# A ten-sublayer transformer on one core: the last two output slots of each sublayer in four quarters, and the next input prepared by token halves

## The chip, the cores and the metric

One core of one Trainium2 chip runs the whole program. The metric is the device time in microseconds (us) of one execution. The core has TensorE (PE, with its weight loads PEld), VectorE (DVE), ScalarE (ACT), GpSimd (POOL) and SyncE (SP, which here only issues DMAs).

## The reference

256 tokens of width 1024 pass through ten sublayers. Each ends in the same way: a product with an output weight matrix, a residual and a layer norm.

```python
for i in range(DEPTH):                       # sublayers 0 to 3
    h = x * (1.0 + scale) + shift            # modulation from c
    y = windowed_gqa(...) if i == 0 else recurrent_block(...)
    x = layer_norm(DN_ALPHA * x + (1.0 + gate) * y, ln_g[i, 0], ln_b[i, 0])
    y = sq_relu_mlp(x * (1.0 + scale) + shift, mlp_w1[i], mlp_w2[i])
    x = layer_norm(DN_ALPHA * x + (1.0 + gate) * y, ln_g[i, 1], ln_b[i, 1])
for i in range(DEPTH):                       # sublayers 4 to 9
    x = layernorm(DN_ALPHA_2 * x + 0.5 * swiglu(x, ...), ...)
    x = layernorm(DN_ALPHA_2 * x + hybrid_mixer(x, ...), ...)
    x = layernorm(DN_ALPHA_2 * x + 0.5 * swiglu(x, ...), ...)
```

So sublayer 0 is attention, 2 a recurrence, 1 and 3 are MLPs, 5 and 8 mixers, and 4, 6, 7 and 9 gated MLPs. "Boundary s" is the place between sublayer s and s + 1.

## The kernel before

**Precision by parts.** Every large product is made of three: each operand is split into a high part (rounded) and a low part (what is left), and `mm3` (L490 to L492) multiplies high by high, low by high and high by low. ScalarE makes the high part of the weights (`weights_hi`, L948) and VectorE the low part (`weights_lo`, L1289), one slot of up to 128 x 2048 at a time.

**Slots.** All weights come in numbered slots. SyncE loads them into three raw buffers; three high and three low buffers follow. A slot is 48 matmuls over 256 columns (`cols_slot`, which needs the transposed input) or 24 over 512 (`rows_slot`, which adds into `y_rows`, 256 tokens as two halves t of 128). High parts are made two slots ahead, but at the end of a sublayer only the next sublayer's first slot is made before the norm; its second and third come after the input's preparation, since ScalarE and VectorE work in the order in which the program is written.

**The end of a sublayer.** `rows_slot` of the last slot runs half 0 (twelve matmuls) and then half 1, and signals `y_half` between them. `norm` on VectorE takes each half: in sublayers 0 to 3 a product with the gate (L1455) and a sum with the scaled residual `x_scaled` (L1457), otherwise one operation (L1459); then statistics (L1463, L1465), a sum with the epsilon and a reciprocal (L1466, L1467). ScalarE takes the root and scales half 0 (L1083 to L1089); VectorE scales half 1 (L1470).

**The preparation of the next input** (`prep`). TensorE transposes the rows (L581), eight blocks of 128 x 128 for each half, into four banks that hold both halves. Banks 0 and 2 are modulated by VectorE (L1390, 256 columns each time), 1 and 3 by ScalarE (L990). ScalarE makes the high part in four pieces (L996), VectorE the low part in four (L1382, `xl_ready` 0 to 3). The first slot goes through its products by input block and waits for each `xl_ready`.

**GpSimd** makes `x_scaled` for the next residual, three operations over 128 x 1024 for each half (L1787, L1789, L1791), as soon as that half's rows are ready (`xn_ready0`, `xn_ready1`). At boundary 0 these lie between loads of the modulation's weights.

**The modulation.** In sublayers 0 and 1 VectorE also accumulates the product of c with the weights `ada_w` (L1339), and TensorE sums it over partitions (`ada_reduce`, L556). In `mlp(1)` the last of these stands at i = 16. Sublayer 2 begins on VectorE with 20 small operations on `rnn_decay_cols` (96 x 32) that wait for each other, with one exponential on ScalarE among them; the low weights of its second slot stand behind them.

Of the kernel before, what the change touches and what calls it, by code (L numbers as in the profile page):

```python
# [27 lines left out]
P = 128  # L28
S = 256
# [67 lines left out]
def build(nc, I, C, out, counts, n_sub):  # L97
# [5 lines left out]
    with ctx:  # L103
# [68 lines left out]
        pos["at"] += 64  # L172
        hid_at = pos["at"]
# [23 lines left out]
        XTF = put("xt", [P, KC, S], at=hid_at)  # L197
# [271 lines left out]
        def _(pe):  # L469
# [51 lines left out]
            def rows_slot(label, lh, ll, k0, first, last, s):  # L521

                n, wh, wl = open_slot(label)
                for t in range(NT):
                    for kk in range(2):
                        xa, xb = lh(k0 + kk)[:, t * P:(t + 1) * P], ll(k0 + kk)[:, t * P:(t + 1) * P]
                        for h in range(2):
                            ins = mm3(Y[:, t, h * 512:(h + 1) * 512], xa, xb, wh[:, kk, h * 512:(h + 1) * 512],
                                      wl[:, kk, h * 512:(h + 1) * 512], first and kk == 0, last and kk == 1)
                    if last and t == 0:  # L530
                        ins.then_inc(*inc("y_half", s))
                ins.then_inc(*inc("rows_done", label))

# [6 lines left out]
            def xready(s):  # L540
                seen = set()

                def f(k):
                    if k // 2 not in seen:
                        seen.add(k // 2)
                        pe.wait_ge(*past("xl_ready", (s, k // 2)))
                return f
# [22 lines left out]
            def prep(s):  # L570

                banks = [topen(("xt", s, e), "AD"[e % 2 == 0]) for e in range(4)]
                for t in range(NT):
                    if s > 0:
                        pe.wait_ge(*past(f"xn_ready{t}", (s - 1, t)))
                    elif t == 0:
                        pe.wait_ge(*past("x_in"))
                    for e in range(4):
                        for kk in range(2):
                            k = 2 * e + kk  # L580
                            ins = pe.transpose(banks[e][:, kk * S + t * P:kk * S + (t + 1) * P], XN[:, t, k * P:(k + 1) * P],  # L581
                                               IDN[:, :])
                        if t == 1:
                            ins.then_inc(*inc("tile_done", ("xt", s, e)))
# [12 lines left out]
            prep(0)  # L597
# [65 lines left out]
            for i in range(4):  # L663
                if i == 1:
                    ada_reduce(5)
                rows_slot((0, "out", i), lambda k: OH[:, k, :], lambda k: OL[:, k, :], 2 * i, i == 0, i == 3, 0)
# [19 lines left out]

            def hidden_rows(s, i, n):
# [3 lines left out]
                hh, hl = HH[:, i % 2, :], HL[:, i % 2, :]  # L691
                rows_slot((s, "w2", i), lambda k: hh.rearrange("p (a b) -> p a b", a=2)[:, k],
                          lambda k: hl.rearrange("p (a b) -> p a b", a=2)[:, k], 0, i == 0, i == n - 1, s)
# [10 lines left out]

            def between(s):

                if s + 1 < n_sub:
                    prep(s + 1)

            def recurrence(s):  # L710
# [4 lines left out]
                for i in range(12):  # L715
# [14 lines left out]
                    if g >= 0:  # L730
                        pe.wait_ge(*past("yl", g))
                        if g == 0:
                            y_wait(s)
                        rows_slot((s, "out", g), lambda k: YH[:, g % 4, k, :], lambda k: YL[:, g % 4, k, :], 0, g == 0, g == 7, s)

            def mixer(s):
# [180 lines left out]
                for i in range(4):  # L917
# [3 lines left out]
                    rows_slot((s, "out", i), lambda k: XH[:, k, :], lambda k: XL[:, k, :], 2 * i, i == 0, i == 3, s)  # L921

            between(0)
            for s in range(1, n_sub):
# [8 lines left out]
                between(s)  # L933
# [3 lines left out]
        def _(act):  # L937
# [42 lines left out]
            def prep(s):  # L980
# [4 lines left out]
                def modulate(e):  # L985

                    bank = tile(("xt", s, e))
                    for kk in range(2):
# [967 lines left out]
```

## Time and profile before

| | |
|---|---|
| median of 3 runs | 2641.73 us (2641.48 to 2643.64) |
| span of the profiled execution | 2640.4 us |
| TensorE busy | 2375.5 us, 90% |
| TensorE weight loads | 2143.8 us, 81% |
| VectorE busy | 1675.4 us, 63% |
| ScalarE busy | 1117.3 us, 42% |
| GpSimd busy | 498.6 us, 19% |
| mean granted clock of TensorE | 0.935 |

The profiled execution's own time is its span and what lies around it. The chain of work that ended last is TensorE for 73% and VectorE for 21% of the span. In the tables below a time is the start from the beginning of the span, and the second number is how long the instruction or the group (xN) took; in brackets stands how long the engine was idle before it, and what ended that.

### The profile page before, as it was taken

The numbers are of one execution on the slowest core, as the hardware profiler recorded it, in microseconds if no ns is written. First come the engines' busy times: TensorE is split into PE (matmuls) and PEld (weight loads), VectorE is DVE, ScalarE is ACT, GpSimd is POOL, SyncE is SP. The second block draws the span as 40 slices with busy tenths as digits, with TensorE's granted clock in tenths as the row PEclk, the third lists the DMA queues.
The fourth block names the chain that finished last, engine by engine and source line by source line (L and its number), as shares of the span: only waits on it lengthen the run. The fifth ranks groups of instructions, "written<-read, shape, count | busy, mean of one in ns | idle before, by whom it ended". The sixth has DMA issues, their size and how long they took to land.

```text
span 2640.4 us, 37438 instructions
## 1 busy us (share of the span) xinstructions
PE 2375.5 (90%) x15755; PEld 2143.8 (81%) x15755; DVE 1675.4 (63%) x1946; ACT 1117.3 (42%) x1452; POOL 498.6 (19%) x379
## 2 busy tenths in 40 slices
PE   4879997886999899899899889999989899889998
PEld 4668887764898899888698789989988778788997
DVE  6977765798655644599544564464467964447544
ACT  2334433665444444455333344343445553234343
POOL 2112113332200200345022020020032522112000
PEclk9889998888899899999898999999999998898999
DMA  9768873223455456545221155555564442013652
GB/s 321 250 210 275 291 244 93 84 76 103 163 188 176 161 187 180 163 129 138 67 65 49 66 174 190 178 172 179 191 142 152 127 115 64 23 59 128 209 186 101
DMA packets 304282, 400.47 MB, mean 152 GB/s; under 512 B 43215, under 2 KB 262969, under 8 KB 304116
## 3 DMA queue, kind: packets, MB, share of 16 engines
q1 hardware_dynamic: 283360, 336.75, 40.2%
q0 software_dynamic: 17504, 57.89, 6.9%
q10 hardware_dynamic: 3252, 3.45, 0.4%
q8 instruction: 125, 2.05, 0.3%
q14 instruction: 41, 0.34, 0.0%
HBM read 393.86 MB, written 4.19 MB: 151 GB/s over the span
## 4 chain that ended last, share of the span: by engine, by line
PE 73%; DVE 21%; ACT 3%; issue 2%; DMA 1%; POOL 0%; SPq 0%; ACTq 0%; DVEq 0%; POOLq 0%
PE tiles L490 14%; PE tiles L491 14%; PE tiles L492 14%; PE y_rows L490 6%; PE y_rows L491 6%; PE y_rows L492 6%; DVE conv_qkv_t L1609 3%; DVE weights_lo L1289 3%; PE tiles L845 2%; PE tiles L859 2%; PE tiles L855 1%; PE tiles L829 1%; DVE xt_lo L1382 1%; DVE ada_acc L1339 1%; DVE rnn_conv_out L1548 1%
## 5 line engine op out<-in xcount | busy, mean ns | idle before, releaser
L1289 DVE TENSOR_TENSOR weights_lo<-weights_raw,weights_hi 128x2048 fp32r<-128x2048 f32 (+2 forms) x316 | 740.2, 2347 | 530.3 <-ACT weights_hi L948 529.9
L490 PE MATMUL tiles<-xt_hi,weights_hi 128*128 128x256 f32 (+1 forms) x3216 | 930.4, 289 | 33.0 <-DVE xt_lo L1382 24.5
L491 PE MATMUL tiles<-xt_lo,weights_hi 128*128 128x256 f32 (+1 forms) x3216 | 921.2, 286 | 0.0
L492 PE MATMUL tiles<-xt_hi,weights_lo 128*128 128x256 f32 (+1 forms) x3216 | 920.3, 286 | 0.0
L948 ACT ACTIVATE weights_hi<-weights_raw 128x2048 fp32r<-128x2048 f32 (+2 forms) x316 | 593.0, 1880 | 218.6 <-PE y_rows L492 191.2
L490 PEld LDWEIGHTS tiles<-xt_hi,weights_hi 128*128 128x128 f32 (+1 forms) x3216 | 621.7, 193 | 52.0 <-issue 38.2
L491 PEld LDWEIGHTS tiles<-xt_lo,weights_hi 128*128 128x128 f32 (+1 forms) x3216 | 622.0, 193 | 3.3
L492 PEld LDWEIGHTS tiles<-xt_hi,weights_lo 128*128 128x128 f32 (+1 forms) x3216 | 621.1, 193 | 0.0
L490 PE MATMUL y_rows<-weights_hi,hid_hi 128*128 128x512 f32 x608 | 244.0, 401 | 0.0
L491 PE MATMUL y_rows<-weights_lo,hid_hi 128*128 128x512 f32 x608 | 242.7, 399 | 0.0
L492 PE MATMUL y_rows<-weights_hi,hid_lo 128*128 128x512 f32 x608 | 242.5, 399 | 0.0
L1787 POOL TENSOR_TENSOR x_scaled<-x_rows,ln_gb_rows 128x1024 f32<-128x1024 f32 x18 | 44.5, 2474 | 873.9 <-ACT x_rows L1089 873.1
L952 ACT ACTIVATE hid_act<-tiles 128x512 f32<-128x512 f32 x76 | 45.5, 598 | 277.6 <-PE tiles L492 277.6
L490 PEld LDWEIGHTS y_rows<-weights_hi,hid_hi 128*128 128x128 f32 x608 | 115.8, 191 | 33.6 <-issue 6.0
L1914 POOL TENSOR_TENSOR l_level_t<-l_t,levels_t 128x512 f32<-128x512 f32 x56 | 76.1, 1359 | 344.2 <-DVE a_t L1682 200.3
L492 PEld LDWEIGHTS y_rows<-weights_hi,hid_lo 128*128 128x128 f32 x608 | 115.5, 190 | 28.3
L491 PEld LDWEIGHTS y_rows<-weights_lo,hid_hi 128*128 128x128 f32 x608 | 115.3, 190 | 25.0
L1339 DVE SCALAR_TENSOR_TENSOR ada_acc<-ada_ring,c_cols,ada_acc 128x1024 f32<-128x1024 f32 x84 | 108.5, 1292 | 17.3 <-DMA ada_ring<-in_ada_w_dram 12.5
L1609 DVE SCALAR_TENSOR_TENSOR conv_qkv_t<-conv_in,conv_cols,conv_qkv_t 128x256 f32<-128x256 f32 x144 | 104.5, 766 | 7.7 <-ACT conv_qkv_t L1169 5.8
L1038 ACT ACTIVATE hid_hi<-hid_val 128x512 fp32r<-128x512 f32 x44 | 27.8, 632 | 181.1 <-DVE hid_val L1508 181.1
L1825 POOL DMA_DIRECT2D ada_ring<-in_ada_w_dram x76 | 40.7, 535 | 267.6 <-DVE ada_acc L1339 221.3
L581 PE MATMUL tiles<-ident,x_rows 128*128 128x128 f32 x160 | 34.8, 391 | 49.7 <-ACT x_rows L1089 27.8
(334 smaller groups left out, 3320.5 us busy)
## 6 DMA issues: line engine op xcount, KB each, us to landing
weights_raw<-in_ffn_w_dram SPq DMA_DIRECT2D x132, 1024.0 KB, 5.1
weights_raw<-in_mlp_w_dram SPq DMA_DIRECT2D x64, 1024.0 KB, 5.8
weights_raw<-in_w_in_dram SPq DMA_DIRECT2D x52, 1024.0 KB, 5.4
ada_ring<-in_ada_w_dram POOLq DMA_DIRECT2D x76, 512.0 KB, 4.9
weights_raw<-in_rnn_w_in_dram SPq DMA_DIRECT2D x16, 768.0 KB, 4.8
ada_ring<-in_ada_w_dram SPq DMA_DIRECT2D x20, 512.0 KB, 7.7
weights_raw<-in_w_in_dram SPq DMA_DIRECT2D x32, 256.0 KB, 4.4
weights_raw<-in_w_branch_a_dram SPq DMA_DIRECT2D x32, 256.0 KB, 4.6
```

What stands on the lines that cost most here:

```text
L490: pe.matmul(o, a, c, start=first, stop=False)
L491: pe.matmul(o, a, d, start=False, stop=False)
L492: return pe.matmul(o, b, c, start=False, stop=last)
L845: ins = pe.matmul(bank[:, j * P:(j + 1) * P], MM[:, c, j, :], TT[:, c, j, :], start=True, stop=True)
L859: ins = pe.matmul(bank[:, j * P:(j + 1) * P], XX[:, c, j, :], UU[:, c, j, :], start=True, stop=True)
L948: act.activation(slot_view(WHI, m, NSPL), slot_view(RAW, m, NRAW), ACT.Copy).then_inc(*inc("hi_ready", m))
L952: act.activation(dst, src, func, **kw).then_inc(*inc("free_A", label))
L1289: dve.tensor_tensor(slot_view(WLO, m, NSPL), slot_view(RAW, m, NRAW), slot_view(WHI, m, NSPL).bitcast(F32), ALU.subtract).then_inc(*inc("l ...
L1339: ins = dve.scalar_tensor_tensor(ACC[:, t % 3, :], ADR[:, m % NADR, :], CC[:, kc:kc + 1], ACC[:, t % 3, :], ALU.mult, ALU.add)
L1609: ins = dve.scalar_tensor_tensor(CB[:, ct, :], CIN[:, j % 2, jj, tap:tap + S], w, CB[:, ct, :], ALU.mult, ALU.add)
L1787: chain(pool.tensor_tensor(XS[:, t, :], XN[:, t, :], GB[:, 0, :], ALU.mult))
L1914: pool.tensor_tensor(MM[:, c, :, :], LT[:, c, :, :], lev, ALU.mult).then_inc(*inc("m_ready", (k_, i, c)))
```

## The change

1. `rows_slot` is used for all output slots but the last two of a sublayer, a and b. These go through `rows_tail`: a and b of half 0 (then `y_half`), a and b of half 1's first 512 columns (`y_third`), a of its other 512 columns, the transposes of half 0, b of those columns, the transposes of half 1. The last two slots' inputs are therefore waited for at other places: in `mlp` and `ffn` nothing of the slot before the last is run until the loop's last turn, and in `mlp(1)` the last `ada_reduce` stands ahead of both.
2. `prep` works by halves: each half has one bank of four blocks for ScalarE and one for VectorE, modulated in pieces of 128 columns; high and low parts are made in four pieces by half and by four blocks. `xl_ready` has two steps, each after the piece of half 1.
3. `norm`: ScalarE takes the root of variance plus epsilon (a new constant), VectorE the reciprocal, and VectorE scales both halves. Half 1's residual and statistics are made in two pieces of 512 columns. VectorE's preparation stands behind half 1's norm; ScalarE's part for half 0 stands ahead of half 1's root. In the last sublayer scaling, gain and shift are two operations for each half.
4. GpSimd's copies wait for the last `xl_ready` of the next sublayer.
5. `xt` lies 8 KB further on, clear of the hidden layer's parts.

```diff
             def rows_slot(label, lh, ll, k0, first):
...
+            def rows_tail(s, a, b, b_ready):
+
+                la, lb = a[0], b[0]
+                for h in range(2):
+                    rows_part(*a, False, False, 0, h)
+                b_ready()
+                for h in range(2):
+                    ins = rows_part(*b, False, True, 0, h)
+                ins.then_inc(*inc("y_half", s))
+                rows_part(*a, False, False, 1, 0)
+                rows_part(*b, False, True, 1, 0).then_inc(*inc("y_third", s))
+                rows_part(*a, False, False, 1, 1).then_inc(*inc("rows_done", la))
+                if s + 1 < n_sub:
+                    prep(s + 1, 0)
+                rows_part(*b, False, True, 1, 1).then_inc(*inc("rows_done", lb))
+                if s + 1 < n_sub:
+                    prep(s + 1, 1)
...
             def hidden_rows(s, i, n):
-                pe.wait_ge(*past("hid_ready", (s, i)))
+
+                if i < n - 1:
+                    pe.wait_ge(*past("hid_ready", (s, i)))
                 if i == 0:
                     y_wait(s)
...
+                if i < n - 2:
+                    rows_slot(*hidden(s, i), i == 0)
+                elif i == n - 1:
+                    rows_tail(s, hidden(s, i - 1), hidden(s, i), lambda: pe.wait_ge(*past("hid_ready", (s, i))))
...
             def prep(s):
...
+                modulate(s, 0)
+                x_lo(s, 0, 0)
+                modulate(s, 1)
+                x_lo(s, 1, 0)
+                x_lo(s, 0, 1)
+                x_lo(s, 1, 1)
...
             def norm(s):
...
+                residual(s, 0, 0, D)
+                for h in range(2):
+                    ins = dve.bn_stats(ST[:, 0, h, :], XN[:, 0, h * 512:(h + 1) * 512])
+                chain(ins)
+                variance(s, 0)
+                scale_rows(s, 0)
+                dve.wait_ge(*past("y_third", s))
+                residual(s, 1, 0, 512)
+                dve.bn_stats(ST[:, 1, 0, :], XN[:, 1, 0:512]).then_inc(*inc("ln_part", s))
+                dve.wait_ge(*past(*y_end[s]))
+                residual(s, 1, 512, D)
+                dve.wait_ge(*past("ln_part", s))
+                chain(dve.bn_stats(ST[:, 1, 1, :], XN[:, 1, 512:D]))
+                variance(s, 1)
+                scale_rows(s, 1)
                 if s + 1 < n_sub:
                     prep(s + 1)
...
             def scaled(s):
 
                 pool.wait_ge(*past("gb_in", s))
+                pool.wait_ge(*past("xl_ready", (s + 1, 1)))
```

**On TensorE at the end of sublayer 1.** The hidden layer's last block, the position of the modulation's reduction (`ones,ada_acc`) and the two output slots. Before:

```order
L683 MATMUL tiles<-bucket_hot,rel_bias 128x384
L490 MATMUL y_rows<-weights_hi,hid_hi 128x512
L491 MATMUL y_rows<-weights_lo,hid_hi 128x512
L492 MATMUL y_rows<-weights_hi,hid_lo 128x512
...
L556 MATMUL tiles<-ones,ada_acc 128x1 x8
L490 MATMUL y_rows<-weights_hi,hid_hi 128x512
...
L581 MATMUL tiles<-ident,x_rows 128x128 x16
L490 MATMUL tiles<-xt_hi,weights_hi 96x256
```

After:

```order
L708 MATMUL tiles<-bucket_hot,rel_bias 128x384
L582 MATMUL tiles<-ones,ada_acc 128x1 x8
L491 MATMUL y_rows<-weights_hi,hid_hi 128x512
L492 MATMUL y_rows<-weights_lo,hid_hi 128x512
...
L606 MATMUL tiles<-ident,x_rows 128x128 x8
L491 MATMUL y_rows<-weights_hi,hid_hi 128x512
...
L606 MATMUL tiles<-ident,x_rows 128x128 x8
L491 MATMUL tiles<-xt_hi,weights_hi 96x256
```

The reduction moved from between the two output slots to ahead of both, and six output matmuls now stand between the two groups of transposes.

**On VectorE at boundary 1,** from half 1's statistics to the start of sublayer 2's decay columns. Before:

```order
L1463 BN_STATS ln_stats<-x_rows 128x6
L1465 BN_AGGR ln_mean_var<-ln_stats 128x2 [waits dve_chain]
L1466 TENSOR_SCALAR ln_rstd<-ln_mean_var 128x1 [waits dve_chain]
L1467 RECIPROCAL ln_rstd<-ln_rstd 128x1 [waits dve_chain]
L1470 TENSOR_SCALAR x_rows<-x_rows,ln_mean_var,ln_rstd 128x1024 [waits ln_rstd]
L1390 TENSOR_SCALAR xt<-tiles,prep_scale,prep_shift 128x256 [waits tile_done]
L1390 TENSOR_SCALAR xt<-tiles,prep_scale,prep_shift 128x256
L1390 TENSOR_SCALAR xt<-tiles,prep_scale,prep_shift 128x256 [waits tile_done]
L1390 TENSOR_SCALAR xt<-tiles,prep_scale,prep_shift 128x256
L1382 TENSOR_TENSOR xt_lo<-xt,xt_hi 128x512 [waits xh_ready] x4
L1531 TENSOR_SCALAR rnn_decay_cols<-rnn_gate_cols 96x32
```

After:

```order
L1538 BN_STATS ln_stats<-x_rows 128x6 [waits ln_part,dve_chain]
L1505 BN_AGGR ln_mean_var<-ln_stats 128x2 [waits dve_chain]
L1510 RECIPROCAL ln_rstd<-ln_rstd 128x1 [waits ln_std]
L1513 TENSOR_SCALAR x_rows<-x_rows,ln_mean_var,ln_rstd 128x1024 [waits dve_chain]
L1418 TENSOR_SCALAR xt<-tiles,prep_scale,prep_shift 128x128 [waits tile_done]
L1418 TENSOR_SCALAR xt<-tiles,prep_scale,prep_shift 128x128 x3
L1426 TENSOR_TENSOR xt_lo<-xt,xt_hi 128x4x128 [waits xh_ready]
L1418 TENSOR_SCALAR xt<-tiles,prep_scale,prep_shift 128x128 [waits tile_done]
L1418 TENSOR_SCALAR xt<-tiles,prep_scale,prep_shift 128x128 x3
L1426 TENSOR_TENSOR xt_lo<-xt,xt_hi 128x4x128 [waits xh_ready] x3
L1595 TENSOR_SCALAR rnn_decay_cols<-rnn_gate_cols 96x32
```

The modulations became eight of half the width, and one low piece stands among them; the decay columns follow directly on the last low piece, as before.

## Rows read from the trace of the kernel before

**Rows 1.** waits of TensorE: engine, tile, line <- released by: us in all, times, longest

```profile
PE tiles L581 <- ACT x_rows L1089: 27.8, 9, 3.8
PE tiles L490 <- DVE xt_lo L1382: 24.5, 10, 3.7
PE tiles L490 <- DVE weights_lo L1289: 7.4, 5, 4.2
```

**Rows 2.** timeline at boundary 4: start us, us, engine, line, operation

```profile
1057.65 1.23 DVE L1459 SCALAR_TENSOR_TENSOR x_rows<-y_rows,x_scaled 128x1024 f32<-128x1024 f32 x1 [2.92 <-PE y_rows L492]
...
1060.01 0.40 PE L492 MATMUL y_rows<-weights_hi,hid_lo 128*128 128x512 f32 x1
1060.23 0.21 DVE L1465 BATCH_NORM_AGGREGATE ln_mean_var<-ln_stats 128x2 f32<-128x12 f32 x1
...
1064.19 1.62 DVE L1470 TENSOR_SCALAR x_rows<-x_rows,ln_mean_var,ln_rstd 128x1024 f32<-128x1024 f32 x1 [0.27 <-ACT ln_rstd L1083]
1065.86 1.97 PE L581 MATMUL tiles<-ident,x_rows 128*128 128x128 f32 x8 [1.03 <-DVE x_rows L1470]
...
1069.83 0.55 PE L490 MATMUL tiles<-xt_hi,weights_hi 128*128 128x256 f32 x1 [2.00 <-DVE xt_lo L1382]
...
1078.49 0.39 PE L490 MATMUL tiles<-xt_hi,weights_hi 128*128 128x256 f32 x1 [1.26 <-DVE weights_lo L1289]
```

**Rows 3.** stretch 1069 to 1073: us; busy (instructions) of each engine; clock; DMA; GB/s

```profile
1069.00:1073.00 4.00, 3.17 (x15) 3.20 (x16) 3.75 (x4) 4.00 (x7) 3.92 (x2) 0.50 0.02 4
```

**Rows 4.** timeline of GpSimd and VectorE at boundary 5

```profile
1550.75 2.77 POOL L1791 TENSOR_SCALAR x_scaled<-x_scaled 128x1024 f32<-128x1024 f32 x1
1551.23 1.10 DVE L1382 TENSOR_TENSOR xt_lo<-xt,xt_hi 128x512 fp32r<-128x512 f32 x1
1553.60 2.52 POOL L1787 TENSOR_TENSOR x_scaled<-x_rows,ln_gb_rows 128x1024 f32<-128x1024 f32 x1
1553.79 2.88 DVE L1382 TENSOR_TENSOR xt_lo<-xt,xt_hi 128x512 fp32r<-128x512 f32 x1
```

**Rows 5.** groups by line and shape: busy us, mean ns of one | idle before

```profile
L1707 DVE TENSOR_SCALAR x_level<-tiles,g_cols 128x128 f32<-128x128 f32 x32 | 8.6, 341 | 0.0
L1390 DVE TENSOR_SCALAR xt<-tiles,ln_cols 128x256 f32<-128x256 f32 x24 | 11.4, 536 | 4.7 <-PE tiles L581 4.7
L990 ACT ACTIVATE xt<-tiles,ln_cols 128x256 f32<-128x256 f32 x24 | 12.2, 562 | 18.5 <-PE tiles L581 18.5
```

**Rows 6.** timeline at boundary 1

```profile
387.60 2.67 DVE L1339 SCALAR_TENSOR_TENSOR ada_acc<-ada_ring,c_cols,ada_acc 128x1024 f32<-128x1024 f32 x2
392.06 1.17 PE L556 MATMUL tiles<-ones,ada_acc 128*128 128x1 f32 x10
...
419.25 0.70 DVE L1531 TENSOR_SCALAR rnn_decay_cols<-rnn_gate_cols 96x32 f32<-96x32 f32 x1
...
427.96 0.53 PE L490 MATMUL tiles<-xt_hi,weights_hi 128*96 128x256 f32 x1 [4.21 <-DVE weights_lo L1289]
```

**Rows 7.** timeline at boundary 0

```profile
163.75 2.67 DVE L1339 SCALAR_TENSOR_TENSOR ada_acc<-ada_ring,c_cols,ada_acc 128x1024 f32<-128x1024 f32 x2
...
177.62 1.97 PE L581 MATMUL tiles<-ident,x_rows 128*128 128x128 f32 x8 [2.35 <-DVE x_rows L1470]
```

**Rows 8.** timeline at boundaries 2 and 3

```profile
650.65 1.23 DVE L1455 TENSOR_TENSOR x_rows<-y_rows,gate_rows 128x1024 f32<-128x1024 f32 x1 [2.78 <-PE y_rows L492]
662.72 1.97 PE L581 MATMUL tiles<-ident,x_rows 128*128 128x128 f32 x8 [3.62 <-DVE x_rows L1470]
...
851.63 1.23 DVE L1455 TENSOR_TENSOR x_rows<-y_rows,gate_rows 128x1024 f32<-128x1024 f32 x1 [3.01 <-PE y_rows L492]
863.70 1.97 PE L581 MATMUL tiles<-ident,x_rows 128*128 128x128 f32 x8 [3.62 <-DVE x_rows L1470]
```

**Rows 9.** timeline at the start and at the end

```profile
49.49 0.55 PE L490 MATMUL tiles<-xt_hi,weights_hi 128*128 128x256 f32 x1 [1.66 <-DVE xt_lo L1382]
...
2636.01 1.22 DVE L1478 TENSOR_TENSOR x_rows<-x_rows,ln_gb_rows 128x1024 f32<-128x1024 f32 x1
```

More of the change, by code:

```diff
@@ L172, in build @@
         pos["at"] += 64
+        EPS = put("ln_eps", [P, 1])
         hid_at = pos["at"]
@@ L519, in v_slot, with rows_slot @@
                 ins.then_inc(*inc("tile_done", label))
-            def rows_slot(label, lh, ll, k0, first, last, s):
+            def rows_slot(label, lh, ll, k0, first):
                 n, wh, wl = open_slot(label)
@@ L596, in _ @@
                 ada_reduce(t)
-            prep(0)
+            for t in range(NT):
+                prep(0, t)
             for i in range(6):
@@ L916, in mixer @@
                     cols_slot((s, "bb", i), OH, OL, "D", ready=(lambda k: pe.wait_ge(*past("olb_ready", (s, k // 2)))) if i == 0 else None)
-                for i in range(4):
+                for i in range(3):
                     pe.wait_ge(*past("ml_ready", (s, i)))
@@ L932, in _ @@
                     ffn(s)
-                between(s)
         @block.scalar
@@ new lines, in residual @@
+            def residual(s, t, c0, c1):
+                x, y = XN[:, t, c0:c1], Y[:, t, c0:c1]
+                last = c1 == D
+                if s < 4:
+                    dve.tensor_tensor(x, y, GATE[:, c0:c1], ALU.mult).then_inc(*(inc("y_free", (s, t)) if last else inc("y_gated", (s, t))))
+                    dve.wait_ge(*past(*(("y_free", (s, t)) if last else ("y_gated", (s, t)))))
+                    chain(dve.tensor_tensor(x, x, XS[:, t, c0:c1], ALU.add))
+                else:
+                    ins = dve.scalar_tensor_tensor(x, y, 1.0 if is_mix(s) else 0.5, XS[:, t, c0:c1], ALU.mult, ALU.add)
+                    if last:
+                        ins.then_inc(*inc("y_free", (s, t)))
+                        dve.wait_ge(*past("y_free", (s, t)))
+                    else:
+                        chain(ins)
@@ new lines, in variance, with scale_rows @@
+            def variance(s, t):
+                dve.bn_aggr(MV[:, t, :], ST[:, t, :, :].rearrange("p a b -> p (a b)")).then_inc(*inc("ln_var", (s, t)))
+            def scale_rows(s, t):
+                dve.wait_ge(*past("ln_std", (s, t)))
+                chain(dve.reciprocal(RV[:, t, 0:1], RV[:, t, 1:2]))
+                x = XN[:, t, :]
+                if s + 1 < n_sub:
+                    dve.tensor_scalar(x, x, MV[:, t, 0:1], RV[:, t, 0:1], ALU.subtract, ALU.mult).then_inc(*inc(f"xn_ready{t}", (s, t)))
+                else:
+                    chain(dve.scalar_tensor_tensor(x, x, MV[:, t, 0:1], GB[:, 0, :], ALU.subtract, ALU.mult))
+                    dve.scalar_tensor_tensor(x, x, RV[:, t, 0:1], GB[:, 1, :], ALU.mult, ALU.add).then_inc(*inc("out_rows", t))
@@ L1471, in norm @@
                 if s + 1 < n_sub:
                     prep(s + 1)
-                else:
-                    dve.wait_ge(*past("gb_in", s))
-                    for t in range(NT):
-                        dve.wait_ge(*past(f"xn_ready{t}", (s, t)))
-                        chain(dve.tensor_tensor(XN[:, t, :], XN[:, t, :], GB[:, 0, :], ALU.mult))
-                        dve.tensor_tensor(XN[:, t, :], XN[:, t, :], GB[:, 1, :], ALU.add).then_inc(*inc("out_rows", t))
             def lo_hidden(s, i):
@@ L1776, in _ @@
             chain(pool.memset(ESEL[:, :], 0.0))
+            chain(pool.memset(EPS[:, :], LN_EPS))
             pool.memset(ESEL[:, 15:16], 1.0).then_inc(*inc("ones_ready"))
```

187 lines of the change are left out of this document (88 added, 99 removed).

## The prediction

> **What bounds the kernel now.** TensorE is busy for 90% of the span, so a change off its path is worth nothing, and one on it is worth what TensorE waited. I read the views in this order. First the waits of TensorE [rows 1]: of its idle time 27.8 us stand in front of the transposes of the normalised rows and 24.5 us in front of a sublayer's first matmul, both at the nine places where one sublayer ends and the next begins; 7.4 us stand in front of a second slot whose low weights are late. Then one such place in order of time, 4 to 5 [rows 2]: from the last output matmul (1060.01) to the first matmul of the next sublayer (1069.83) lie 9.8 us, a chain of small steps on VectorE and ScalarE, and then the second slot waits until 1078.49. Then the clock there [rows 3]: the first slot after the pause runs at 0.50 of full speed, the 1.2 GHz level, after an engine that had mostly waited since 1060.4.
>
> **The lock.** GpSimd's copies (six of about 2.5 us at each boundary) and VectorE's reads exclude each other [rows 4]: the low part of the input started at 1553.79 while a GpSimd tensor_tensor ran from 1553.60 to 1556.12, and ended at 1556.67, though it takes 0.65 alone. Under GpSimd's tensor_scalar (from 1550.75) the same operation took 1.10: this form blocks only in pieces. The Trainium skill (SBUF — State Buffer, "Who interferes with whom") says that the loser of this port fully blocks for the whole instruction; by that rule, the trace agrees for tensor_tensor and not for tensor_scalar.
>
> **Boundaries 4 to 8 (no gate).** Count from the start S of the last two slots: 48 matmuls at 0.233 us, so S = 1060.01 - 47 x 0.233 = 1049.05. Before, the chain of half 0 starts at 8.6 [rows 2], after 36 matmuls; now after 24, at 5.8. VectorE has its last weights work done 2.9 before 1057.65, at 5.7: just free. The chain takes 2.58 to the variance [rows 2], then 0.21, root 0.24, reciprocal 0.21, scaling 0.85 (the row's 1.62 has a wait for GpSimd in it, which is now silent): 4.1, so 9.9. TensorE has run 42 matmuls by then (9.8): no wait. Eight transposes 1.0, the last six matmuls 1.4: the last starts at 12.1, not 11.0. Half 1's first columns are done meanwhile; its second columns start 0.45 later and take 0.7 residual, 0.7 statistics, 0.24, 0.24, 0.21, 0.85: rows ready at 15.5, where before they were at 16.8 (1065.86).
> Then the preparation. It now has 4 + 4 modulations of 128 columns for each half. VectorE's 256-column form takes 536 ns and a 128-column one 341 [rows 5]; back to back I take 1.2 for four. ScalarE's 562 ns has no 128-column row: between half of it and all of it; I take 0.39 each back to back, 1.56 for four, since its fixed part stays. The chain is VectorE modulation of half 0 (1.2), ScalarE high part (0.65), ScalarE modulation of half 1 (1.5), high part (0.65), VectorE low part (0.7), TensorE (0.15): 4.85, against 3.97 before. First matmul at 20.35 against 20.8: **0.4 less**, five times, 2.2. The second slot's wait for low weights, 7.4 in all less 4.2 at boundary 1 [rows 1, 6], goes: 3.2 more. It should go because the high part is ready 6.5 after the transposes start and a copy holds VectorE until 8.6, so low weights are there at 10.8, and TensorE needs them at 12 to 13.4 (its first slot takes 7.1 to 8.6 at these clocks). Sum **-5.4**.
>
> **Boundary 3 (gate, free GpSimd contention before).** The gate adds 1.26 to the chain of half 0 (5.4) and makes half 1's tail 4.15. S = 851.63 - 8.6 = 843.03 [rows 8]. Rows 0 at 11.2, so TensorE waits 1.4; last matmul 13.35; rows 1 at 17.5 = 860.5, against 863.70. The preparation took 5.7 before, with copies running through it; now 4.85. **-4.0.**
> **Boundary 2** is held by the recurrence's last step: the chain of half 0 starts at 650.65 in both. Then 656.05, 658.2, 662.35 against 662.72 [rows 8]; with the preparation's 0.8, **-1.2**. Three quarters of the two slots' work now stand behind that step, which eats the rest.
> **Boundary 0.** The chain can't start 2.8 earlier, since VectorE has two accumulations of the modulation until 166.42 [rows 7]: 166.45 + 5.4 + 2.2 + 4.15 = 178.15 against 177.62, and no copies disturbed it before, so its preparation took 3.6: 4.85 now. **+1.8.** At the **start** both halves are turned at once (from 44.2), and the narrower steps put the first matmul at 51.1 instead of 49.49 [rows 9]: **+1.6**.
> **The end.** Scaling and the last weights and biases become two operations for each half instead of three, the first half's done while the second runs: 2622.3 + 3.3 + 2.6 = 2628.2, then 2 x 1.4, 0.7 and 2.6 = 2634.3, against 2637.2 [rows 9]: **-2.9**.
>
> **Boundary 1** is where the change costs. Two things move. (a) TensorE's reduction of the modulation stands ahead of both slots, not between them; it needs the accumulation that ends at 390.27 and ran at 392.06, hidden [rows 6]. Now TensorE waits for it, and S is 390.3 + 1.75 = 392.05; rows 1 at 409.55, the input complete at +6.15 = 415.7. (b) Behind the input VectorE has 20 small dependent operations for the decay columns, then the low weights; from 419.25 to TensorE's restart at 427.96 they took 8.7 [rows 6], with the copies over. Now the copies start at the same moment, and 18 of the 20 read two operands or go in the form that the lock stops. Between two copies passes one of them (0.2), since GpSimd takes the port while the next waits for its predecessor. Step by step from 0: copy to 2.55, one operation, ScalarE's table and exponential to 4.45, copy to 5.4, one; tensor_scalar 5.5 to 8.3, of whose middle 1.2 us are free: six; copy to 10.85, one; copy to 13.65, one; tensor_scalar to 16.5: six; the rest and the low weights (1.76): 18.8. TensorE at 434.5 instead of 427.96: **+6.6**. Bounds: no blocking at all, 423.9, a gain of 4.0; both tensor_scalars blocking throughout, 436.5, +8.6.
>
> **Sum:** 1.6 + 1.8 + 6.6 - 1.2 - 4.0 - 5.4 - 2.9 = -3.5. The profiled execution has a span of 2640.4, and the median of the runs is 2641.7, so 1.3 lie around the span and move with nothing here: **2638.2 us**. GpSimd's own later work (clearing the convolution's input, bias rows) starts some 7 us later at each boundary, several slots before its first reader: I take nothing. Later slots: I followed the lock through four slots and found low weights 1 to 5 us ahead.
>
> **Rivals.**
> *The small operations slip through* (B): if GpSimd lets VectorE go on between copies, boundary 1 gains 4 and the time is 2638.2 - 10.6 = 2627.6. For it: 128x1 operations pass in any case. Against: the row at 1553.79. Chance 0.14.
> *The lock takes the second slot* (C, slower): low weights at each of boundaries 2 to 8 are caught by two copies instead of one, because the port is given to GpSimd again. They then come 2.65 later, at 13.4, or 0.6 after the mean need of 12.8, and each later slot's low weights are as late; with the 3.2 us not gained and one further copy (0.6 x 7 = 4.2, up to 2.6 lost for the ones behind) the time is 2638.2 + 3.2 + 4.2 + 2 = 2647.6. It decides when the low weights are more than 12.8 behind the transposes. Chance 0.15.
> *Narrow is not cheaper* (D): if 128 columns cost as 256 do, 0.7 on VectorE and 0.3 on ScalarE are added at nine preparations: 2647. Against: 341 against 536 ns. Chance 0.06.
> *The page's lock* (E): tensor_scalar blocks throughout and boundary 1 costs 8.6: 2640.2. The sentence of the Trainium skill above states it. Against: the 1.10 us row. Chance 0.10.
> *The clock rises sooner* (F): the transposes and matmuls between the pauses keep the 2.4 GHz level; a first slot lost about 2 us to the lower level, so half of that at eight boundaries gives 2630. For it: TensorE's pauses are now two of 3 us. Against: pauses of 2.5, 1 and 2 us already brought the lower level. Chance 0.10.
> My forecast (A) holds the other 0.45, of which 0.12 lie more than 5.3 us below the median.
>
> **How the numbers follow.** 0.2% (5.3 us) is about what a measurement can tell from no change. Faster: B, F and 0.12 of A, 0.36. Slower: C, D, 0.21, less what of them stays inside, 0.20. Same: 0.44. The range leaves out B's end and C's tail: 2629 to 2647.
>
> **What would show it.** Two transposes of eight with six output matmuls between them, without a wait at 4 to 8 and with 1.4 us at 3. Scaling at 0.81 throughout. At boundary 1 the reduction waiting about 4 us, decay operations strung between copies, and a wait of some 12 us for low weights. No other wait for low weights at a second slot. Wrong would be: first matmuls less than 0 or more than 1.5 us earlier at 4 to 8, or a boundary 1 that is no later.

## The result and the profile after

The changed kernel takes 2647.0 us (median of 20 runs, 2645.5 to 2650.8), the kernel before 2642.6 (20 runs, 2640.6 to 2647.7): ratio 1.0016, 95% interval 1.0009 to 1.0022. That is inside the 0.2% called no change, but slower, where 3.5 us less was forecast, and 0.01 us outside the range. The profiled execution's span is 2645.3, 4.9 longer than before.

The waits of TensorE after (engine, tile, line, releaser: us in all, times, longest) answer to [rows 1]:

```profile
PE tiles L606 <- DVE x_rows L1513: 39.1, 18, 3.9
PE tiles L491 <- DVE xt_lo L1426: 35.1, 10, 3.7
...
PE tiles L491 <- DVE weights_lo L1323: 7.8, 1, 7.8
```

The waits at the boundaries grew (39.1 for 27.8, 35.1 for 24.5), but work stands between them now; the low weights keep TensorE waiting at one place instead of five. Boundary 4 in order of time, the timeline of TensorE, VectorE and GpSimd together (start, us, engine, line, operation), answers to [rows 2]:

```profile
1047.62 0.40 PE L491 MATMUL y_rows<-weights_hi,hid_hi 128*128 128x512 f32 x1
...
1053.29 1.23 DVE L1496 SCALAR_TENSOR_TENSOR x_rows<-y_rows,x_scaled 128x1024 f32<-128x1024 f32 x1
...
1057.51 1.10 PE L606 MATMUL tiles<-ident,x_rows 128*128 128x128 f32 x8 [0.18 <-DVE x_rows L1513]
...
1059.61 0.40 PE L493 MATMUL y_rows<-weights_hi,hid_lo 128*128 128x512 f32 x1
...
1062.27 0.81 DVE L1513 TENSOR_SCALAR x_rows<-x_rows,ln_mean_var,ln_rstd 128x1024 f32<-128x1024 f32 x1
...
1063.14 1.09 PE L606 MATMUL tiles<-ident,x_rows 128*128 128x128 f32 x8 [3.13 <-DVE x_rows L1513]
...
1067.95 0.55 PE L491 MATMUL tiles<-xt_hi,weights_hi 128*128 128x256 f32 x1 [3.72 <-DVE xt_lo L1426]
...
1069.15 2.38 POOL L1852 TENSOR_TENSOR x_scaled<-x_rows,ln_gb_rows 128x1024 f32<-128x1024 f32 x1 [174.26 <-DVE xt_lo L1426]
```

This is the picture that was forecast: eight transposes and six matmuls without a wait worth the name, scaling at 0.81, 4.81 from the transposes to the first matmul (4.85 forecast), copies behind it, no wait in the second slot. And yet two numbers don't fit. Eight transposes were put ahead of the last matmul, but it comes at 1059.61, not later than 1060.01. And what boundaries 2 to 8 gained is gone by the end.

I followed the shift against before from boundary to boundary, at the 240th matmul behind the last transpose of the rows. The last column is a later experiment (the hidden tiles put where they were against 64 bytes).

| part | forecast | after | after_unaligned |
|---|---|---|---|
| start and boundary 0 | +3.4 | +5.2 | +5.0 |
| boundary 1 | +6.6 | +3.7 | +6.8 |
| boundary 2 | -1.2 | -2.5 | -2.0 |
| boundary 3 | -4.0 | -6.8 | -4.4 |
| boundaries 4 to 8 | -5.4 | -14.2 | -9.8 |
| the two mixers (sublayers 5, 8) | 0 | +23.6 | +23.6 |
| end | -2.9 | -4.1 | -3.0 |
| sum | -3.5 | +4.9 | +16.1 |

So the size of the miss isn't 8 us. Two unforeseen terms, -10 and +21, stand against each other. (The mixers' row holds 2 x 1.1 for the later last matmul, which the forecast has at the boundaries. Two expectations below have 3.8 up to sublayer 1 and 5.0 for boundary 1; on the same matmul in both kernels it is 5.2 and 3.7.)

**The mixers.** The stretch from the long wait in front of the attention rows to the last output matmul of sublayer 8, in both kernels (us, busy of PE, PEld, DVE, ACT and POOL with their instructions, granted clock, DMA share, GB/s). Before:

```profile
2028.00:2427.00 399.00, 364.03 (x2521) 324.28 (x2521) 251.83 (x427) 159.62 (x276) 96.16 (x68) 0.92 0.30 91
```

After:

```profile
2029.00:2439.00 410.00, 375.57 (x2529) 334.07 (x2528) 253.38 (x429) 161.68 (x281) 95.12 (x67) 0.90 0.30 89
```

The same work (eight transposes more, about 1 us) keeps TensorE busy 11.5 us longer, at a mean granted clock of 0.90 for 0.92. It doesn't wait longer: the waits for attention rows have the same lengths (the two longest 3.05 and 2.15 us before, 3.06 and 2.15 after) and add up to 26.5 both times. Summed over the clock records, a whole mixer sublayer, the 5th or the 8th, spends 71.7 us at the 1.2 GHz level before and 92.2 after; the 20.5 us between them cost half, 10.3, of the 11.8 that it takes longer from its 240th matmul on. The changed code comes behind all of this: only the tail and GpSimd's times differ ahead of it.

Where the level falls differs, even at the same place of the program and of the span. Before, the first attention matmul behind the long wait, and the stretch at the lower level next to it:

```profile
2028.79 0.90 PE L759 MATMUL y_rows<-ident,probs_a 128*128 128x128 f32 x3 [3.05 <-DVE probs_a L1599]
2028.80:2032.20 3.40, 3.40 (x14) 2.74 (x15) 3.40 (x2) 2.29 (x2) 1.06 (x1) 0.50 0.02 5
```

After:

```profile
2028.80 0.90 PE L794 MATMUL y_rows<-ident,probs_a 128*128 128x128 f32 x3 [3.06 <-DVE probs_a L1663]
2027.30:2034.20 6.90, 5.40 (x23) 4.74 (x24) 6.83 (x9) 3.09 (x7) 2.49 (x2) 0.51 0.20 46
```

Both waits end 2028.8 us into the span. Before, the lower level starts with the first matmul behind the wait (the 6.8 us ahead of it are at 1.00); after, 1.4 us ahead of it, and it stays twice as long.

### The profile page after: what moved, and what is told of

Same layout as the page of the kernel before. It is cut to its first block, busy times and chain, and to the rows that moved or that the text cites. A ratio compares the mean times of both kernels' runs of the same rounds, so it can differ in the third digit from the quotient of the medians.

```text
span 2645.3 us, 37493 instructions
## 1 busy us (share of the span) xinstructions
PE 2375.2 (90%) x15755; PEld 2153.1 (81%) x15755; DVE 1693.3 (64%) x1988; ACT 1116.3 (42%) x1462; POOL 525.3 (20%) x380
## 4 chain that ended last, share of the span: by engine, by line
PE 74%; DVE 19%; ACT 3%; issue 2%; DMA 1%; POOL 0%; SPq 0%; ACTq 0%; DVEq 0%; POOLq 0%
PE tiles L491 15%; PE tiles L492 14%; PE tiles L493 14%; PE y_rows L491 6%; PE y_rows L492 6%; PE y_rows L493 6%; DVE conv_qkv_t L1673 3%; DVE weights_lo L1323 2%; PE tiles L880 2%; PE tiles L894 2%; PE tiles L890 1%; PE tiles L864 1%; DVE ada_acc L1373 1%; DVE rnn_conv_out L1612 1%; DMA ada_ring<-in_ada_w_dram 1%
## 5 line engine op out<-in xcount | busy, mean ns | idle before, releaser
L1323 DVE TENSOR_TENSOR weights_lo<-weights_raw,weights_hi 128x2048 fp32r<-128x2048 f32 (+2 forms) x316 | 767.7, 2434 | 508.5 <-ACT weights_hi L984 508.2
L491 PE MATMUL tiles<-xt_hi,weights_hi 128*128 128x256 f32 (+1 forms) x3216 | 929.0, 289 | 43.9 <-DVE xt_lo L1426 35.1
L1075 ACT ACTIVATE hid_hi<-hid_val 128x512 fp32r<-128x512 f32 x44 | 27.8, 632 | 179.7 <-DVE hid_val L1572 179.7
L1546 DVE TENSOR_TENSOR hid_lo<-hid_val,hid_hi 128x512 fp32r<-128x512 f32 x76 | 57.5, 757 | 32.1 <-ACT hid_hi L1075 30.8
```

The costliest lines, as they stand in the source:

```text
L491: pe.matmul(o, a, c, start=first, stop=False)
L1323: dve.tensor_tensor(slot_view(WLO, m, NSPL), slot_view(RAW, m, NRAW), slot_view(WHI, m, NSPL).bitcast(F32), ALU.subtract).then_inc(*inc("l ...
L1546: dve.tensor_tensor(HL[:, i % 2, :], VB[:, i % 2, :], HH[:, i % 2, :].bitcast(F32), ALU.subtract).then_inc(*inc("hid_ready", (s, i)))
```

## The experiments

Theory A is the forecast's: the order and the lock. G: the late copies put GpSimd's later work in the mixer's way. P: where a mixer's pauses fall against the changes of the granted clock decides its time, not its code. H, formed later: the place of a tile. Each ratio is against the kernel before on the same chip.

**1. The two parts apart.** In the changed kernel the copies are set free again:

```
-                pool.wait_ge(*past("xl_ready", (s + 1, 1)))
...
-                pool.wait_ge(*past("xl_ready", (1, 1)))
```

> The changed kernel without the two waits that keep GpSimd's copies behind the next input: the copies start when the normalised rows are there, as in the kernel before. Theory A (the copies' lock is what boundary 1 pays for, and what the later boundaries gained): boundary 1 loses its 5.0 us again, and boundaries 2 to 8 give back about 1.6 us each (scaling at 1.6 instead of 0.85, low weights late at the second slot), 11 in all; start and end as in the changed kernel. If the mixers keep their longer time (11.8 us each), that gives 2647 + 6 = 2653. Rival G (the mixers are longer because the copies and what follows them on GpSimd run 7 us later in them): the mixers lose 23 us and the time is near 2630. The mixers' time between the boundaries tells them apart: 11.8 longer than before each, or as before.

2660.6 us, 1.0062 (1.0049 to 1.0075), 7.6 more than theory A's 2653: boundary 1 lost its 4.0 us, but boundaries 2 to 8 gave back 15, not 11. And the kernel before with only the copies late (the same two waits, on `xl_ready` 3):

> The kernel before with only the copies moved behind the next input's low part. Theory A: boundary 1 loses about 6 us (decay operations between copies), and boundaries 2 to 8 gain: scaling of half 1 without the lock (0.8), the preparation of boundary 3 without copies (1.5), no late weights at second slots (3.2 in all): about 9 less, so 2642.6 + 6 - 9 = 2640. Rival G: each mixer takes some 12 us longer than before, 2664. Rival P (the mixers' time hangs on where their pauses fall against the changes of the clock, not on the code): mixers anywhere from 0 to 12 us longer, with the same waits.

2640.1 us, 0.9995 (0.9983 to 1.0006). Theory A gave the time, for a wrong reason: without the mixers (+8.3 and +11.9 at the same places) this kernel is 23 us faster, and boundary 1, where 6 was charged, costs 0.4, since its input is ready 4.1 earlier. G falls: the mixers are 11.7 and 12.0 longer with early copies, too. What the copies do when they are early, in the timeline of copies_early at boundary 4:

```profile
1071.92 2.35 POOL L1852 TENSOR_TENSOR x_scaled<-x_rows,ln_gb_rows 128x1024 f32<-128x1024 f32 x1
1074.35 2.71 POOL L1854 TENSOR_TENSOR x_scaled<-x_scaled,ln_gb_rows 128x1024 f32<-128x1024 f32 x1
1077.14 3.10 POOL L1856 TENSOR_SCALAR x_scaled<-x_scaled 128x1024 f32<-128x1024 f32 x1
...
1073.24 5.81 DVE L1426 TENSOR_TENSOR xt_lo<-xt,xt_hi 128x512 fp32r<-128x512 f32 x3 [0.60 <-ACT xt_hi L1031]
```

Three low parts take 5.8 us instead of 1.9. From boundary 2 to 8 the copies' move alone gains 23 us; the new tail and preparation alone (copies_early) 9, of which 6 turn out below to be something else. Part of the 23 is clock: outside the mixers 176 us are spent at the lower level, for 199 before, and half of that difference is 11 us, an upper bound (where TensorE waits, the level costs nothing). And on top of late copies the new order doesn't gain at all: from the last output matmul to the first of the next sublayer boundary 4 takes 9.82 us before [rows 2], 8.55 in before_copies_late, and 8.34 in the changed kernel, whose last matmul comes 1.1 later. A wider preparation (3.51 from the transposes, for 4.81) and undisturbed copies do in the old order what the halves were to do.

**2. Boundary 1.** The changed kernel with `if s != 1:` ahead of the wait in `scaled`:

> The changed kernel, with the copies at boundary 1 alone put back in front of the next input. Theory A: of the 5.0 us that boundary 1 costs (from 3.8 to 8.9 later at the 240th matmul) the late copies cost 4.0, as in the kernel with all copies early, so the 240th matmul of sublayer 2 comes 4 us earlier than in the changed kernel; boundary 2 can't keep all of it, since the recurrence there ends by its own chain, and I expect 3 us at the end: 2644, mixers 491.5 as before. If boundary 1 loses by something else (the reduction ahead of both slots, the new preparation), no change: 2647.

2643.5 us, 0.9998 (0.9989 to 1.0007), 3.5 less than the changed kernel. The boundary gains 0.3 instead of costing 3.7. The late copies and the decay columns in the changed kernel:

```profile
421.19 2.41 POOL L1852 TENSOR_TENSOR x_scaled<-x_rows,ln_gb_rows 128x1024 f32<-128x1024 f32 x1 [43.74 <-DVE xt_lo L1426]
423.69 2.41 POOL L1854 TENSOR_TENSOR x_scaled<-x_scaled,ln_gb_rows 128x1024 f32<-128x1024 f32 x1
...
424.06 2.09 DVE L1582 TENSOR_TENSOR rnn_decay_cols<-rnn_decay_cols 96x32 f32<-96x32 f32 x1
...
427.34 1.52 DVE L1586 SCALAR_TENSOR_TENSOR rnn_decay_cols<-rnn_decay_cols 96x32 f32<-96x32 f32 x7
...
436.80 0.53 PE L491 MATMUL tiles<-xt_hi,weights_hi 128*96 128x256 f32 x1 [7.76 <-DVE weights_lo L1323]
```

A 0.2 us operation that meets a copy is held for its rest (2.09), and under GpSimd's tensor_scalar seven pass in a row, in the 1.52 us that they take in boundary1_copies_early with no copy beside them: the pieces of [rows 4]. The copies' lock is what the sum charged.

**3. The mixers, moved.** VectorE computes a low part again, two, three or four times (0.7 us each), at the start of the two mixers only; nothing later changes:

```
                 x_lo(s, 0, 0)
                 modulate(s, 1)
+                for _ in range(2 if is_mix(s) else 0):
+                    chain(dve.tensor_tensor(XL[:, 4:8, 0:P], XTF[:, 0:4, 0:P], XH[:, 0:4, 0:P].bitcast(F32), ALU.subtract))
```

> The changed kernel, but at the start of the two mixer sublayers (5 and 8) VectorE computes a low part twice more, which puts the input 0.6 to 1.4 us later and changes nothing else. Rival P (the extra 11.8 us of each mixer are TensorE at its lower clock level, set by where the pauses fall): the time at the lower level in a mixer moves away from 92 us, towards 72, and the kernel gets faster by up to 20 us in spite of the delay. Theory A and rival G: 1 to 3 us slower than the changed kernel, 2648 to 2650, the mixers' time at the lower level stays at 92 us.

> The changed kernel with three extra low-part operations of VectorE at the start of each mixer sublayer. Two gave mixers of 494.9 and 489.8 us, four gave 498.4 twice, none gives 491.5. Theory P (where the pauses of a mixer fall against the changes of the granted clock decides how much of it runs at the lower level): three put the mixer's pauses nearly where the kernel before has them (its first low stretch starts within 0.3 us of the 3 us wait in front of the attention values), so mixers of about 484.5 (482.6 and the delay), 61 to 65 us at the lower level behind that wait, and 2647 - 14 = 2633 for the kernel. A theory in which the delay only adds: 497, and 2658.

> As the last one with four of these operations, 2.0 to 2.8 us later. Rival P: again another time at the lower level than 92 us; if it follows only the place and the place repeats, near the one of the kernel before (72), and the kernel near 2632. Others: 4 to 6 us slower than the changed kernel, 2651 to 2653, and 92 us at the lower level.

2649.6 (1.0024), 2654.5 (1.0034) and 2661.4 us (1.0065). The mixers themselves, from the last output matmul ahead of one to its own: 491.5 and 491.7 us without delay; 494.9 and 489.8 with two; 493.2 and 495.6 with three; 498.3 and 498.5 with four. So their time moves with their start, in steps that are not the delay (one of them fell), and in two kernels the two mixers, which run the same code, differ. The time at the lower level leaves 92 us (95.6 and 85.3 with two, 92.2 and 99.0 with three, 102.4 twice with four), as P has it, but not towards 72: P's faster kernels didn't come, and with two operations the kernel's time alone is the one that A and G gave. My forecast for three, back to 484.5, was wrong: P says that the place decides, but I couldn't tell from one low stretch where a shifted mixer would land. The direct test is the kernel before with two such operations, 1.4 us:

> The kernel before with two extra low-part operations of VectorE (1.4 us) at the start of each mixer sublayer and nothing else. Theory P: its mixers lose their favourable place: from that wait in front of the attention values to the last output matmul 406 to 413 us where the kernel before takes 397.9, and the kernel 2642.6 + 2 x (1.4 + 8 to 15) = 2662 to 2675. If the mixers of the changed kernels are longer for a reason in their code: 2642.6 + 2.8 = 2645.4, and 398 us.

2668.5 us, 1.0089 (1.0073 to 1.0104): 24 us for 2.8 us of delay, without any code of the change. Its mixer:

```profile
1145.00:1556.00 411.00, 375.00 (x2521) 333.91 (x2521) 251.72 (x428) 159.46 (x275) 93.83 (x68) 0.90 0.29 88
```

It has the 2521 instructions of before and the busy time and clock of after. P stands. In all thirteen kernels whose mixers' pauses were left empty, the stretch behind that wait takes 397.9 to 414.0 us, and less half of its time at the lower level 365.4 to 368.7. The clock records of these 26 stretches also say which place is the good one. In three of them (both mixers of the kernel before, one of before_aligned below) the lower level starts between 0.0 ahead of and 0.6 us behind the first attention matmul after the long wait, and the stretch has 61 to 65 us of it; in the other 23 it starts 0.3 to 1.6 us ahead or 1.3 to 1.7 behind, and they have 78 to 92. That is a pattern in the records; no experiment set that place by itself. With the copies late in the kernel before and the same two operations:

> The kernel before with only the copies moved, which took 2640.1 with mixers of 488.2 and 491.7, and now with the same two extra operations at the start of the mixers. Theory P: the mixers' pauses move by 1.4 us to the favourable place: 484 each, and the kernel 2640.1 - (4 + 8) = 2628; by the theory of added delay 2643.

2645.8 us, 1.0004 (0.9995 to 1.0013), mixers of 495.4 and 490.0: another aim missed. The lower level starts 0.6 us ahead of that matmul in the first mixer and 1.7 behind it in the second.

**4. The pauses, filled.** TensorE turns the identity in front of the waits for attention rows, the inverse and the output norm, into the tile that is opened anyway:

```
+                        fill(bank, 0 if c else 18)
                         pe.wait_ge(*past("u0_ready", (k_, c)))
```

> The changed kernel with TensorE kept busy in the mixers' pauses: in front of nine waits for attention rows (4 to 16 extra 128x128 transposes of the identity, 0.125 us each at full clock, into the tile that is opened anyway), of the wait for the inverse's start (18, in both halves) and of the wait for the output norm (16); no pause is filled beyond about three quarters. Theory P (the mixer is 11.8 us longer because more of it runs at the lower level after its pauses): the 92 us at the lower level fall to 40 to 60, a mixer takes 475 to 485 instead of 491.5, and the kernel 2615 to 2635. If the lower level isn't set by the pauses: 92 us and up to 5 us longer, 2650.

> The kernel before with the same filled pauses in its mixers. Theory P: it gains less than the changed kernel does, since its mixers ran only 72 us at the lower level; both end within 4 us of each other in the mixers (475 to 485), so 2627 to 2645 here, and the difference of the two kernels turns over: the changed one 10 to 20 us faster. If the mixers differ by something else, they stay 9 us apart in length, and the kernels 4 us.

2640.7 (0.9993) and 2644.5 us (1.0011). The order of the two kernels turns over, but by 3.9 us, not 10 to 20, and the changed kernel stays above the 2615 to 2635 expected. A mixer of the changed kernel spends 68.3 us at the lower level, for 92.2, and takes 488.6, for 491.5: of 12 us that the clock gives back the extra work takes 9. The 63 transposes in front of the attention rows, about 8 us of work, leave 8.8 us of waits there where 13.3 stood, since new waits of 1.1 to 1.8 us come up between them; and the 18 in front of the inverse run in part at the lower level (3.05 and 2.37 us). The rest I didn't trace. The filled kernel before has 58.0 and 54.6, and takes 484.5 and 482.9, no less than the 482.6 and 482.5 without filling. Two more kernels with filled mixers, the second with boundary 1's early copies and filled boundaries:

> The kernel before, copies late, with the same filled pauses. Without them 2640.1, of which 20 us were the mixers' longer time. Theory P: 2610 to 2628, the copies' move alone being worth some 20 us against the filled kernel before. Otherwise 2640 to 2645.

> The changed kernel, boundary 1's copies early (2643.5 us so), the mixers' pauses filled, and at boundaries 3 to 8 14 transposes in front of half 1's and 16 in front of the next sublayer's first matmul. Theory P: the first slots no longer run at 0.50 of full clock, 1 to 2 us less at each of six boundaries on top of the mixers: 2600 to 2625. If the filled work is itself at the lower level, half 1 is turned later by up to 0.4 us and the first matmul by 0.3: no gain there.

2622.9 (0.9936; 0.9914 to 0.9958) and 2633.1 us (0.9964). The first has mixers of 480.3 and 481.5 us, for 488.2 and 491.7 unfilled. The second misses its 2600 to 2625: its mixers take 488.8 and 486.5, and the filled boundaries bring 2 us, not 6 to 12.

**5. The missing microseconds ahead of the last matmul.** In the changed kernel all output matmuls of the MLP and FFN sublayers follow each other after 0.228 us, in long slots that the edit doesn't touch, and before after 0.233. In the mixers' output slots both have 0.227. The edit adds `EPS = put("ln_eps", [P, 1])`, 32 bytes, ahead of `hid_hi` and `hid_lo`. Counted from the first tile, these begin 32 bytes off a multiple of 64 before, and on one after, where `xt_hi` lies anyway. Two kernels move only these and the tiles placed behind them:

```
-        pos["at"] += 64
+        pos["at"] += 96
```

> The kernel before, with nothing changed but the place of the hidden tiles: 32 bytes further on, as the changed kernel's new ln_eps column puts them. Theory H: this alone makes the 1824 output matmuls of the MLP and FFN sublayers 0.2279 us apart instead of 0.2332, 9.7 us in all. Then the mixers: if they keep their 482.5 us, 2633; if the 1.4 us by which each FFN ends earlier moves their pauses (theory P), up to 2 x 12 us more, so 2633 to 2656, with the spacing 0.228 in any case. Rival: the spacing comes from the new order of the tail or the instructions' place; then 0.233 and 2642.6.

In the changed kernel `pos["at"] += 32` stands behind the new column:

> The changed kernel with the hidden tiles 32 bytes further on again, so that they lie as in the kernel before against 64 bytes. Theory H: output matmuls 0.2332 apart, 9.7 us slower, 2657, with mixers that may change their time by up to 12 us each either way (theory P; 491.5 now). That is then what the edit of the order itself does, without the gift of the new column. Rival: 0.228 and 2647.

The first of the 48 matmuls ahead of boundary 4 in the kernel before (the last is in [rows 2]):

```profile
1049.05 0.39 PE L490 MATMUL y_rows<-weights_hi,hid_hi 128*128 128x512 f32 x1
```

First and last in before_aligned:

```profile
1040.32 0.40 PE L490 MATMUL y_rows<-weights_hi,hid_hi 128*128 128x512 f32 x1
...
1051.00 0.39 PE L492 MATMUL y_rows<-weights_hi,hid_lo 128*128 128x512 f32 x1
```

10.68 / 47 = 0.2272, and before it is 10.96 / 47 = 0.2332. The mean over 1100 to 1200 such matmuls is 0.2278 in before_aligned, 0.2333 before, 0.2329 in after_unaligned, 0.2279 after. H holds, for 1824 x 0.0053 = 9.7 us. after_unaligned takes 2659.2 us, 1.0061 (1.0048 to 1.0074), 12 more than the changed kernel. before_aligned takes 2644.8 (1.0006; 0.9994 to 1.0018), no faster, because its mixers are no longer alike:

```profile
1135.00:1535.00 400.00, 364.84 (x2521) 325.24 (x2521) 252.35 (x430) 159.55 (x276) 95.93 (x68) 0.92 0.30 91
2017.00:2426.00 409.00, 373.95 (x2521) 332.20 (x2521) 251.88 (x428) 159.44 (x275) 93.73 (x68) 0.90 0.30 89
```

One execution, one code, 2521 matmuls each: 9 us apart, and its clock with them. Its twelve executions lie between 2639.3 and 2654.0 us, at mean granted clocks from 0.931 down to 0.923, so the same happens with no change of the code at all; the profile shows one of the shortest. The last two put together what was found:

> The kernel before with the copies late (2640.1) and the hidden tiles moved by 32 bytes. Theory H: 9.7 us less, 2630, and by theory P the mixers (488.2 and 491.7 without it) anywhere from 482 to 498: 2620 to 2645.

> The same with the mixers' pauses filled; unaligned it took 2622.9. Theory H: 2613. With filled pauses the mixers took 480 to 489 us in four kernels, so by theory P at most 16 us more: 2613 to 2629, likeliest 2613 to 2618.

2636.9 us (0.9963; 0.9949 to 0.9978), with mixers of 493.8 and 493.7 in the profile of a long execution (two of its seven took 2627.3 and 2627.8, at clocks of 0.932 and 0.933 for 0.927), and 2617.0 us (0.9902; 0.9888 to 0.9915), 30 less than the changed kernel and 26 less than before. The order by halves isn't in it: with unmoved tiles and late copies it takes 2659.2 and the old order 2640.1, 3 of these 19 us in the mixers and 12 at the start and boundaries 0 and 1.

## Why the prediction was wrong

Two steps failed, both terms that the sum has at nothing. The mixers, under "I take nothing" for what comes behind the boundaries, took 21 us more, by TensorE's clock. The new column's effect on where the hidden tiles lie, which the sum doesn't name, gave 9.7 back. With unmoved tiles each row of the boundaries lies within 2.2 us of its forecast. That the measured time lies only 8.8 us from the forecast is luck: the two terms have opposite signs.

- **Start and boundary 0**: +3.4 forecast, +5.2. The start was right (first matmul at 51.00, forecast 51.1; 49.71 in after_unaligned). At boundary 0 half 0's transposes and the last six output matmuls run at the lower level: 1.83 and 2.6 us, where 1.0 and 1.4 were assumed, behind a wait of 2.8.
- **Boundary 1**: right in kind and size. TensorE restarts at 436.80, 8.8 later than before, where 3.4 + 6.6 = 10.0 were charged; with the tiles as before the boundary costs 6.8. Without late copies it costs 4.0 less. Rivals B and E fall: single operations were stopped for up to 2.4 us, and the tensor_scalar let seven pass in 1.5. The wait for low weights is 7.8 us, not some 12. The reduction waits 3.9 (about 4):

```profile
392.67 3.55 PE L582 MATMUL tiles<-ones,ada_acc 128*128 128x1 f32 x16 [3.94 <-issue]
```

- **Boundaries 2 and 3**: -1.2 and -4.0 against -2.0 and -4.4 with unmoved tiles. Right. The MLP of sublayer 3 adds 384 x 0.0053 = 2.0 of its own.
- **Boundaries 4 to 8**: -5.4 against -9.8 with unmoved tiles, and with the 2.2 that stand in the mixers' row -7.6. The earlier first matmul (2.2 forecast, 2.2 unmoved) and the preparation were right to 0.1. Too small was the term for late low weights, 3.2: where the row shows a wait of only 0.3, the first slot ran longer at the lower level (8.3 us, not 7.4) and hid the rest. From the first matmul to the 240th each boundary gained 1.3 to 1.4, 6.7 in all, in the changed kernel, and 5.4 with unmoved tiles. A wait's row tells what it costs beside what runs now, not what is there to win.
- **The end**: -2.9 against -3.0 unmoved. Right.
- **The tile's place**: -9.7, missed. The diff shows one new column ahead of `hid_hi`, and I costed it at nothing. The two columns of the table differ by 11.2; the other 1.5 lie within what the clock explains, since outside the mixers after_unaligned spends 4.6 us more at the lower level.
- **The mixers**: +21, missed; this is the step that turned a gain into a loss. "GpSimd's own later work ... I take nothing" asked the right place the wrong question: nothing there waits longer, but the same work is done at another clock. Rival F had the clock in it, as a gain at eight first slots and nowhere else. Its gain came in part: from the last output matmul to the 240th of the next sublayer each of boundaries 4 to 8 spends 6.8 us at the lower level, for 10.2 before. But before_copies_late has 6.8 there too, in the old order, so the shorter chain brings it and not the matmuls between the pauses. The kernel before has the shortest two such stretches of all the unfilled kernels (398.0 and 397.9; the next is 398.3, and the others are over 406): it had everything to lose.
- **C and D** didn't come: low weights wait nowhere but at boundary 1, and four narrow modulations take 1.36 (1.2 assumed).

What is shown: that the mixers' longer time is TensorE at the lower level, and that a delay at their start brings it about in the old code. What stays open: what sets the moment at which the lower level starts, since I aimed twice and missed, and neither the code nor the time from the span's start decides it; and why the 20 executions of each of the two kernels lie within 5 and 7 us, while those of before_aligned and late_copies_aligned lie 15 and 11 us apart.

## What to carry to other kernels

Cost a move of a second engine's copies by the operations with two inputs that it meets, and leave them early where the chain behind is made of small ones (4.0 us at boundary 1 of the changed kernel; in the old order it made 0.4). Before reading a difference of a few us as the edit's doing, compare the busy time and granted clock of long stretches that it doesn't touch: here the noise that any shift makes (up to 16 us a mixer) is larger than the change. And look at where every tile lies once one is added.

## What the runs showed of the hardware

- fp32r matmuls with a moving operand of 128x512 follow each other after 0.233 us when the tile of the loaded 128x128 operand begins 32 bytes off a multiple of 64 (counted from the first tile), and after 0.228 when it begins on one.
- A shift of 1.4 us at the start of a stage with pauses of 1 to 3 us every 9 us made it 14 us longer, 12 of them behind the first long pause, of which 12.0 and 10.3 in the two mixers are TensorE's clock (half of 23.9 and 20.5 us more at the lower level). The whole kernel before spends 342 us of its span at the 1.2 GHz level and the changed one 365, which costs half of that where TensorE works, at most 6.5 and 6.9%. The Trainium skill (TensorE: Matmul & The Clock Gate, "What's actually happening") puts the penalty of the ramp under 1% of a typical kernel's span. That is a figure for the ramp at a kernel's start; here the level falls again and again throughout the kernel, and the figure doesn't cover it.
- Transposes that fill a pause hold the 2.4 GHz level in part: 24 us less at the lower one in a mixer of the changed kernel, of which 3 us were left as a gain. The same filling gained nothing in the kernel before and 8 to 10 us a mixer with its copies late.
- GpSimd's tensor_tensor of 128x1024 held a 0.19 us operation of VectorE with two inputs for 2.09 us; its tensor_scalar of the same width let seven such pass in 1.52.
